# The gated-delta scan's block inverse as 32x32 and 64x64 tile products, with forward and backward heads in turn

## The chip, the cores and the metric

One core of one Trainium2 chip runs the whole program. The metric is the time of one execution in microseconds on the device. The core's engines are TensorE (PE, matrix products), VectorE (DVE), ScalarE (ACT), GpSimd (POOL) and SyncE (SP); SP and ACT also issue DMAs.

## The reference

The program is a forward pass of a small model on 256 context and 512 latent tokens of width 1024: a mixer layer with an SSD scan and a gated-delta scan in two directions, an output projection and MLP, then two further blocks with attention and gated MLPs. What matters here is the gated-delta scan (8 heads of 128, forward and backward):

```python
def gdn_scan(q, k, v, g, beta, S0, return_y):
    ...
    decay = exp(where(incl, gcum[..., :, None] - gcum[..., None, :], -inf))
    kk = einsum('bchik,bchjk->bchij', k_beta, kc) * decay
    tmat = eye(Q) + where(strict, kk, 0.0)
    rhs = concatenate([vc * bc, k_beta * exp(gcum)[..., None]], axis=-1)
    sol = triangular_solve(tmat, rhs, lower=True, unit_diagonal=True)
    ...
    def step(S, inp):
        v_new = u_i - w_i @ S
        S_next = S * d_i + kd_i^T @ v_new
        o = qd_i @ S + qk_i @ v_new
```

The kernel works in chunks of 128 tokens (6 chunks), so each head and chunk needs the inverse of a 128x128 unit triangular matrix: lower triangular for the forward direction, upper for the backward one.

## The kernel before, in words

The scan lies between the SSD scan and the output projection, from about 665 to 872 us of the span. The 16 pairs of head and direction are handled as four quads q of four heads each. Before, q = 0, 1 are the two head groups forward and q = 2, 3 the two backward. Each quad has its tiles with four 128x128 matrices side by side (128 x 512): `S` the state, `DT0`/`DT1` (one for each parity of the step t) the transposed inverse, `DB` its untransposed diagonal blocks, `C5`/`C6` the off-diagonal corners of the matrix (32x32 corners and the 64x64 corner), `PM` the negated product, `KD`, `VN`, `QE`, `QKD`, `VB` for the scan itself, and two banks of PSUM: `A[q]` for the inverse, `B[q]` for the scan. In traces `DU` is the tile of `DT0`, and `C` stands for both `C5` and `C6`.

The 32x32 diagonal blocks are inverted earlier, and come back through memory. The scan then builds the 128x128 inverse in two levels. For the first, `corner5` multiplies the 32x32 corners with the inverted diagonal blocks, ACT (`corner`) negates the result into `PM`, `block5` multiplies with the other diagonal block, and DVE (`block5`) copies and transposes the blocks that are needed into `DB` and `DT`. The second level, `corner6`, `corner`, `block6_t` and DVE's `block6_t`, does the same with 64x64 blocks. Of each product only off-diagonal blocks are needed, but all four parts call

```python
            def four(dst, w, x):
                for j in range(4):
                    o = slice(j * P, (j + 1) * P)
                    mm = pe.matmul(dst[:, o], w[:, o], x[:, o], start=True, stop=True)
                return mm
```

with whole 128x128 matrices, in which the unneeded blocks of `C5`, `C6` and `DT` are zeros that POOL wrote (`zeroed`).

The inverse of step t + 1 is built within step t. PE's order in a step t is written out by hand: per quad `state_read` and `corner5(t + 1)`; per quad `new_values` and `block5(t + 1)`; the four `output` (latent chunks, t >= 2); per quad `state_step` and `corner6(t + 1)`; per quad `key_rows(t + 1)` (transposes) and `block6_t(t + 1)`; and four `gate_rows`. Step 5, the last, builds nothing. In step 0 `square_sum` products of the SSD norm stand between the `corner5`. ACT's order is: four copies of corner 5, four `new_values`, four copies of corner 6, then `load_corners(t + 2, q)`, three DMAs per quad. DVE's is `right_side`, `block5`, `output`, `state_step`, `key_rows` with `block6_t`, `gated_query`. SP's queue loads, for each t and q, four diagonal blocks into `DT` (`load_dt`, which waits for `new_values` of step t - 2 and `corner5` of t - 1), then three into `DB` (`load_d32`, which waits for `corner6` of t - 1), and after the four quads `VB` and `QKD` for each (`load_step`; `QKD` waits for `output` of the step before, q by q). `corner5(t, q)` waits for all ten small loads of its quad: `pre_loaded[q]` counts them.

Of the kernel before, what the change touches and what calls it, by code (L numbers as in the profile page):

```python
# [18 lines left out]
P = 128  # L19
D = 1024  # L20
# [7 lines left out]
SH = 16  # L28
# [206 lines left out]
def build_kernel(nc, a, out):  # L235
    ctx = ExitStack()
    with ctx:
# [239 lines left out]
        def pair_of(q, t):  # L477

            return (q // 2 * NCH + GSEQ[q // 2][t]) * 2 + q % 2

        def lat_pair(q, t):

            return (q // 2 * (NCH - NCTX) + GSEQ[q // 2][t] - NCTX) * 2 + q % 2

        def block_at(q, t):

            if t < 4:
                return q // 2, (2 * t + q % 2) * 16
            return 2, 64 * (q // 2) + (2 * (t - 4) + q % 2) * 16
# [30 lines left out]
        def scal4(ap, w):  # L520
# [66 lines left out]
            12, 24, 24, 20, 24, 24, 24, 16, 24, 48, 3, 2, 11, 8, 8, 8, 3, 20, 20, 16, 16, 20, 20, 20, 16, 16, 24, 24, 24, 24, 65, 65, 65, 8, 32, 4)  # L587
# [56 lines left out]
        def _(sp_):  # L644
# [87 lines left out]
            for ts, ds in (((0, 1, 2, 3), (0,)), ((0, 1, 2, 3), (1,)), ((4, 5), (0, 1))):  # L732
                for d in ds:
                    for t in ts:
                        for q in (2 * d, 2 * d + 1):
# [36 lines left out]
            def load_d32(t, q):  # L772

                for r in (0, 1, 2) if q < 2 else (1, 2, 3):
                    sp_.dma_start(diagonal(DB[q][:, :], r), blocks_of(xv_dram, q, t, r)).then_inc(pre_loaded[q], 16)

            def load_step(t, q):

                d, c = q // 2, GSEQ[q // 2][t]
# [4 lines left out]
                sp_.dma_start(VB[q][:, :], v_dram[:, c * D + 512 * (q % 2):c * D + 512 * (q % 2) + 512]).then_inc(vb_loaded[q], 16)  # L784
# [17 lines left out]
            for t in range(1, NCH):  # L802
                for q in range(4):
                    if t == 4:
                        sp_.wait_ge(xb_stored, 64)
                        sp_.wait_ge(xv_stored, 64)
                    n = 4 * (t - 1) + q + 1
                    if t == 1:
                        sp_.wait_ge(zeroed, 12 + q + 1)
                    else:  # L810
                        sp_.wait_ge(dr_full, n - 4)
                    sp_.wait_ge(p5_full, n)
                    load_dt(t, q)
                    sp_.wait_ge(p6_full, n)
# [27 lines left out]
        def _(pe):  # L842
# [242 lines left out]
            def key(t, q, j):  # L1085

                h, c = 4 * (q % 2) + j, GSEQ[q // 2][t]
# [9 lines left out]
            def block5(t, q):  # L1097

                pe.wait_ge(pm_ready, 8 * t + q + 1)
                four(A[q], DT[t % 2][q], PM[q]).then_inc(e5_full, 1)  # L1100

            def corner6(t, q):

                pe.wait_ge(dt64_ready, 4 * t + q + 1)
                four(A[q], C6[q], DB[q]).then_inc(p6_full, 1)

            def block6_t(t, q):

                pe.wait_ge(pm_ready, 8 * t + 4 + q + 1)
                four(A[q], PM[q], DT[t % 2][q]).then_inc(e6t_full, 1)  # L1110
# [9 lines left out]
            def gate_rows(t, q):  # L1120
# [5 lines left out]
                pe.matmul(B[q][:, :], rowcol((GSEQ[q // 2][t] - NCTX) * 4 + q), grow[6][:, :], start=True, stop=True).then_inc(egb_full, 1)  # L1126
# [53 lines left out]
            for part in (corner5, block5, corner6, block6_t):  # L1180
                for q in range(4):
                    part(0, q)
            for t in range(NCH):
                lat, more = t >= NCTX, t < NCH - 1
                for q in range(4):
                    if t:
                        state_read(t, q)
                    if more:
                        corner5(t + 1, q)
                    if t == 0:  # L1190
                        if q == 0:
                            pe.wait_ge(kd_ready, 4)
                        for b in ((0, 1, 2), (3, 4, 5), (6, 7), ())[q]:
                            square_sum(b)
                for q in range(4):
                    if t == 0 and q >= 2:
                        pe.wait_ge(norm_ln, q - 1)
                    new_values(t, q)
# [1503 lines left out]
```

## Time and profile before

| what | value |
|---|---|
| median of 3 runs | 2569.04 us (2565.2 to 2571.09) |
| time of the profiled execution | 2571.75 us |
| its span in the profile | 2569.9 us |
| PE busy, share of the span | 94% |
| scan, step 0 to the end of step 5 | 694.64 to 871.99 us |

A span starts with the first instruction and ends with the last; the time of an execution has about 1.9 us more around it. Busy shares count instructions of products, copies and the like, not waits or the issue of DMAs. PEclk or the granted clock is the share of TensorE's full speed that it was given: 1.00 is 2.4 GHz, 0.50 is 1.2 GHz. In traces a float32 product is recorded as two passes, each with a load of the weights ahead of it (PEld), so one `four` is eight records.

### The profile page before, as it was taken

What the parts mean: (1) busy time and instruction counts of PE and PEld (TensorE: products, weight loads), DVE (VectorE), ACT (ScalarE), POOL (GpSimd) and SP (SyncE); (2) the same over time, 40 slices, a digit from 0 to 9 for tenths busy, and PEclk for the clock granted to TensorE, in tenths of its full rate; (3) what the DMA queues carried; (4) which work ended last, traced back from release to release, by engine and by line L of the source; (5) the groups of instructions that cost most, each with busy time, mean ns of one, the idle gap of its engine ahead of it and who ended that gap; (6) DMA issues with size and microseconds to landing.
All of it is one profiled execution on the core that took longest, in us unless ns stands there. A gap on an engine that the chain in (4) does not pass through costs nothing.

```text
span 2569.9 us, 30397 instructions
## 1 busy us (share of the span) xinstructions
PE 2406.2 (94%) x12022; PEld 1942.5 (76%) x12022; DVE 1364.3 (53%) x2161; ACT 1020.2 (40%) x1687; POOL 153.9 (6%) x116
## 2 busy tenths in 40 slices
PE   3899899978899998999999899999999899999997
PEld 2788787734699876888887668888888667888885
DVE  8566774488566534444445654434344554444445
ACT  3544457623432554233255354222235354322222
POOL 0000000000000010000031301000002301000002
PEclk9999999965799999999999999999999999999998
DMA  5233425511343422222232202222223201222222
GB/s 237 99 123 123 164 83 164 190 32 38 89 115 92 152 82 84 99 98 99 91 106 74 66 1 78 97 97 98 99 88 108 66 25 42 98 99 96 93 98 82
DMA packets 124477, 248.29 MB, mean 97 GB/s; under 512 B 58096, under 2 KB 58864, under 8 KB 123568
## 3 DMA queue, kind: packets, MB, share of 16 engines
q1 hardware_dynamic: 106320, 234.02, 27.7%
q10 hardware_dynamic: 18016, 12.33, 1.6%
q8 instruction: 96, 1.57, 0.3%
q14 instruction: 45, 0.37, 0.0%
HBM read 221.13 MB, written 25.17 MB: 96 GB/s over the span
## 4 chain that ended last, share of the span: by engine, by line
PE 81%; DVE 8%; ACT 4%; DMA 3%; issue 2%; ACTq 0%; SPq 0%; POOL 0%; DVEq 0%
PE bank L1219 18%; PE bank L1221 18%; PE bank L1220 18%; PE bank L1082 4%; PE bank L928 4%; PE bank L1379 3%; PE bank L1370 2%; DMA raw<-in_s_qkvx 2%; DVE cacc L2020 2%; PE bank L927 1%; PE bank L392 1%; PE bank L1405 1%; PE bank L394 1%; PE bank L393 1%; DMA modw<-in_w_mod 1%
## 5 line engine op out<-in xcount | busy, mean ns | idle before, releaser
L1666 ACT ACTIVATE whi<-raw 128x1024 fp32r<-128x1024 f32 (+1 forms) x267 | 277.7, 1041 | 927.8 <-PE bank L1221 923.2
L1219 PE MATMUL bank<-ahi,whi 128*128 128x512 f32 x1152 | 454.9, 395 | 9.1 <-DVE alo L2421 6.0
L1220 PE MATMUL bank<-alo,whi 128*128 128x512 f32 x1152 | 451.2, 392 | 0.0
L1221 PE MATMUL bank<-ahi,wlo 128*128 128x512 f32 x1152 | 450.9, 391 | 0.0
L2303 DVE TENSOR_TENSOR wlo<-raw,whi 128x1024 fp32r<-128x1024 f32 (+1 forms) x267 | 326.3, 1222 | 135.4 <-ACT whi L1666 134.9
L1219 PE MATMUL bank<-bhi,whi 128*128 128x512 f32 x736 | 286.8, 390 | 0.0
L1221 PE MATMUL bank<-bhi,wlo 128*128 128x512 f32 x736 | 286.6, 389 | 0.0
L1220 PE MATMUL bank<-blo,whi 128*128 128x512 f32 x736 | 286.6, 389 | 0.0
L1219 PEld LDWEIGHTS bank<-ahi,whi 128*128 128x128 f32 x1152 | 218.0, 189 | 59.2 <-issue 10.6
L1221 PEld LDWEIGHTS bank<-ahi,wlo 128*128 128x128 f32 x1152 | 217.9, 189 | 45.7
L1220 PEld LDWEIGHTS bank<-alo,whi 128*128 128x128 f32 x1152 | 217.8, 189 | 45.8 <-issue 1.4
L2636 POOL TENSOR_TENSOR accx<-accx,sqr 128x512 f32<-128x512 f32 x42 | 72.3, 1721 | 1603.8 <-ACT sqr L1734 1379.7
L1219 PEld LDWEIGHTS bank<-bhi,whi 128*128 128x128 f32 x736 | 138.2, 188 | 28.8 <-issue 0.3
L1221 PEld LDWEIGHTS bank<-bhi,wlo 128*128 128x128 f32 x736 | 138.3, 188 | 28.6
L1220 PEld LDWEIGHTS bank<-blo,whi 128*128 128x128 f32 x736 | 138.3, 188 | 28.6
L2379 DVE TENSOR_TENSOR xr<-bank,xr 128x512 f32<-128x512 f32 x64 | 44.3, 691 | 157.1 <-PE bank L1221 157.1
L409 DVE TENSOR_TENSOR wlo<-raw,whi 128x1024 fp32r<-128x1024 f32 x51 | 62.3, 1222 | 99.2 <-ACT whi L402 98.9
L402 ACT ACTIVATE whi<-raw 128x1024 fp32r<-128x1024 f32 x51 | 54.4, 1068 | 146.6 <-DMA raw<-in_s_qkvx 84.2
L928 PE MATMUL bank<-hhi,whi 128*128 128x512 f32 x272 | 109.8, 404 | 0.0
L928 PE MATMUL bank<-hlo,whi 128*128 128x512 f32 x272 | 109.0, 401 | 0.0
L928 PE MATMUL bank<-hhi,wlo 128*128 128x512 f32 x272 | 108.8, 400 | 0.0
L2020 DVE SCALAR_TENSOR_TENSOR cacc<-cbuf,vec,cacc 128x784 f32<-128x784 f32 (+1 forms) x102 | 98.2, 963 | 10.7 <-ACT cacc L1521 8.0
(421 smaller groups left out, 3974.9 us busy)
## 6 DMA issues: line engine op xcount, KB each, us to landing
raw<-in_s_gu SPq DMA_DIRECT2D x88, 512.0 KB, 3.2
raw<-in_s_qkvx SPq DMA_DIRECT2D x34, 512.0 KB, 4.8
late_modw<-in_w_mod SPq DMA_DIRECT2D x32, 512.0 KB, 3.8
raw<-in_s_up SPq DMA_DIRECT2D x32, 512.0 KB, 3.2
raw<-in_s_down SPq DMA_DIRECT2D x32, 512.0 KB, 3.2
raw<-in_s_dn SPq DMA_DIRECT2D x32, 512.0 KB, 3.2
raw<-in_s_win SPq DMA_DIRECT2D x24, 512.0 KB, 3.2
raw<-in_s_zg SPq DMA_DIRECT2D x16, 512.0 KB, 4.0
```

Of the source, the lines that this page charges most:

```text
L402: act.activation(whi[k][:, 0:kc * P], raw[k][:, 0:kc * P], ACT.Identity).then_inc(hi_ready, 1)
L409: dve.tensor_tensor(wlo[k][:, 0:kc * P], raw[k][:, 0:kc * P], whi[k][:, 0:kc * P].bitcast(F32), ALU.subtract).then_inc(lo_ready, 1)
L928: mm = pe.matmul(lat, w, x[:, s, CTX:TOK], start=first, stop=last)
L1082: mm = pe.matmul(dst[:, o], w[:, o], x[:, o], start=True, stop=True)
L1219: pe.matmul(out, w_hi, x_hi, start=start, stop=False)
L1220: pe.matmul(out, w_hi, x_lo, start=False, stop=False)
L1221: return pe.matmul(out, w_lo, x_hi, start=False, stop=stop)
L1379: mm = pe.matmul(bank[4 + (h // 2) % 2][64 * (h % 2):64 * (h % 2) + 64, qb * P:(qb + 1) * P], vh[:, kb_ * LAT + h * 64:kb_ * LAT + (h + 1) ...
L1666: act.activation(whi[u % 2][:, 0:width[u + 2] * P], raw[u % 2][:, 0:width[u + 2] * P], ACT.Identity).then_inc(hi_ready, 1)
L2020: after(dve.scalar_tensor_tensor(out=acc, in0=x, scalar=w, in1=acc, op0=ALU.mult, op1=ALU.add))
L2303: dve.tensor_tensor(wlo[u % 2][:, 0:width[u + 2] * P], raw[u % 2][:, 0:width[u + 2] * P], whi[u % 2][:, 0:width[u + 2] * P].bitcast(F32), ...
L2636: pool.tensor_tensor(acc[:, :], acc[:, :], sqr[n % 2][:, :], ALU.add).then_inc(sq_added, 1)
```

## The change

All quads are renumbered: q = 0, 2 are now forward and q = 1, 3 backward (q % 2 is the direction, q // 2 the head group). The four inverse parts of PE are issued for pairs of quads p, (0, 1) and (2, 3), one forward and one backward. The first level is made of eight products 32x32 by 32x32 per quad, the second of four 64x64 by 64x64, and the products of the two quads of a pair alternate. As the two directions use opposite corners, neighbouring products lie on different row and column groups of the array. ACT's copy of the second corner covers only its 64x64 blocks. `C5` and `C6` are no longer zeroed, so their loads don't wait for it. SP fetches the `DT` blocks of all four quads before the `DB` blocks of any.

```diff
+            def blocks32(first, w, x, full, p):
+                for j in range(4):
+                    for i in range(2):
+                        for q in (2 * p, 2 * p + 1):
+                            a, b = (2 * i, 2 * i + 1) if q % 2 == 0 else (2 * i + 1, 2 * i)
+                            k, m = (a, b) if first else (b, b)
+                            rows, out = slice(32 * k, 32 * k + 32), slice(32 * b, 32 * b + 32)
+                            mc, nc_ = slice(j * P + 32 * m, j * P + 32 * m + 32), slice(j * P + 32 * a, j * P + 32 * a + 32)
+                            mm = pe.matmul(A[q][out, nc_], w[q][rows, mc], x[q][rows, nc_], start=True, stop=True)
+                            if j == 3 and i == 1:
+                                mm.then_inc(full, 1)
-            def corner5(t, q):
-                pe.wait_ge(pre_loaded[q], 160 * (t + 1))
-                if t:
-                    pe.wait_ge(dt_ready, 4 * (t - 1) + q + 1)
-                four(A[q], C5[q], DB[q]).then_inc(p5_full, 1)
+            def corner5(t, p):
+                for q in (2 * p, 2 * p + 1):
+                    pe.wait_ge(pre_loaded[q], 160 * (t + 1))
+                    if t:
+                        pe.wait_ge(dt_ready, 4 * (t - 1) + q + 1)
+                blocks32(True, C5, DB, p5_full, p)
...
+            def quadrants(upper, w, x, full, p):
+                for j in range(4):
+                    for q in (2 * p, 2 * p + 1):
+                        k, m = (slice(0, 64), slice(64, 128)) if (q % 2 == 0) == upper else (slice(64, 128), slice(0, 64))
+                        kc, mc = slice(j * P + k.start, j * P + k.stop), slice(j * P + m.start, j * P + m.stop)
+                        mm = pe.matmul(A[q][m, kc], w[q][k, mc], x[q][k, kc], start=True, stop=True)
+                        if j == 3:
+                            mm.then_inc(full, 1)
...
                 if more:
-                    for q in range(4):
-                        state_step(t, q)
-                        corner6(t + 1, q)
-                    for q in range(4):
+                    for p in range(2):
+                        state_step(t, 2 * p)
+                        state_step(t, 2 * p + 1)
+                        corner6(t + 1, p)
+                    for p in range(2):
...
             for t in range(1, NCH):
...
                 for q in range(4):
-                    n = 4 * (t - 1) + q + 1
...
                     load_dt(t, q)
-                    sp_.wait_ge(p6_full, n)
+                for q in range(4):
+                    sp_.wait_ge(p6_full, 4 * (t - 1) + q + 1)
                     load_d32(t, q)
...
             def corner(t, q, full):
                 act.wait_ge(full, 4 * t + q + 1)
-                act.activation(PM[q][:, :], A[q][:, :], ACT.Identity, scale=-1.0).then_inc(pm_ready, 1)
+                src, dst = h4(A[q][:, :]), h4(PM[q][:, :])
+                if full is p6_full:
+                    r, c = (slice(64, 128), slice(0, 64)) if q % 2 == 0 else (slice(0, 64), slice(64, 128))
+                    src, dst = src[r, :, c], dst[r, :, c]
+                act.activation(dst, src, ACT.Identity, scale=-1.0).then_inc(pm_ready, 1)
...
             for q in range(4):
-                act.wait_ge(zeroed, 4 + 2 * (q + 1))
                 load_corners(0, q)
...
-            for q in range(4):
-                for t in (C5, C6):
-                    pool.memset(t[q][:, :], 0.0).then_inc(zeroed, 1)
```

DVE's `key_rows` and `block6_t` also go by pairs: two `key_rows`, then two `block6_t`. In step 0 five `square_sum` follow the first pair's `corner5` and three the second's.

## Rows read from the trace of the kernel before

**Rows 1.** The page: span, busy time of TensorE, granted clock in 40 slices.

```profile
span 2569.9 us, 30397 instructions
PE 2406.2 (94%) x12022; PEld 1942.5 (76%) x12022; DVE 1364.3 (53%) x2161; ACT 1020.2 (40%) x1687; POOL 153.9 (6%) x116
PEclk9999999965799999999999999999999999999998
```

**Rows 2.** Stretches: length, busy us of each engine, granted clock, DMA share, GB/s.

```profile
676.20:694.60 18.40, 17.42 (x128) 17.07 (x129) 8.38 (x21) 8.81 (x16) 0.00 (x0) 0.85 0.39 89
694.64:724.69 30.05, 30.05 (x227) 26.23 (x225) 16.23 (x32) 16.34 (x32) 0.00 (x0) 1.00 0.30 62
724.69:753.19 28.50, 28.12 (x247) 27.41 (x245) 18.28 (x56) 9.23 (x24) 0.00 (x0) 1.00 0.60 184
753.19:788.60 35.41, 35.10 (x308) 34.58 (x309) 22.25 (x61) 9.33 (x24) 0.00 (x0) 1.00 0.34 84
857.68:871.99 14.31, 14.31 (x128) 14.31 (x129) 10.95 (x28) 9.01 (x25) 0.00 (x0) 1.00 0.59 200
640.00:660.00 20.00, 19.64 (x112) 10.92 (x110) 16.28 (x46) 9.61 (x33) 0.00 (x0) 0.50 0.01 1
```

**Rows 3.** Timeline of PE in step 2: start us, us, line, what, count.

```profile
774.73 1.06 PE L1082 MATMUL bank<-VN,KD 128*128 128x128 f32 x8
775.62 1.06 PE L1082 MATMUL bank<-DB,C 128*128 128x128 f32 x8
...
787.12 1.18 PE L1126 MATMUL bank<-grow,rowsel 128*128 128x512 f32 x4
788.60 1.16 PE L1137 MATMUL bank<-S,kf 128*128 128x128 f32 x8 [0.31 <-DVE QE L2261]
```

**Rows 4.** Timeline of ACT's DMA issues at the end of step 2.

```profile
782.08 1.20 ACTq L1674 DMA_DIRECT2D C<-at_scratch  x2
...
789.20 0.62 ACTq L1676 DMA_DIRECT2D C<-at_scratch  x1
```

**Rows 5.** Timeline of SP's DMA issues behind step 2's outputs, first and last.

```profile
775.41 1.74 SPq L770 DMA_DIRECT2D DU<-xb_scratch  x4
...
789.97 1.57 SPq L775 DMA_DIRECT2D DB<-xv_scratch  x3
```

**Rows 6.** DMA issues from 665 to 870: count, size, median us to landing.

```profile
C<-at_scratch ACTq DMA_DIRECT2D x24, 64.0 KB, 2.4
DB<-xv_scratch SPq DMA_DIRECT2D x72, 16.0 KB, 2.1
```

**Rows 7.** Timelines of PE and ACT between steps 0 and 1.

```profile
719.37 0.60 PE L1117 MATMUL bank<-cf,kf 128*128 128x128 f32 x4
719.81 1.06 PE L1082 MATMUL bank<-DT,PM 128*128 128x128 f32 x8
...
731.18 1.16 PE L1082 MATMUL bank<-DB,C 128*128 128x128 f32 x8
...
719.58 1.20 ACTq L1674 DMA_DIRECT2D C<-at_scratch  x2
```

**Rows 8.** Timeline of PE in attention, one of its rounds.

```profile
1489.57 0.60 PE L1405 MATMUL bank<-cf,eb 128*128 128x128 f32 x4
1490.10 1.09 PE L1379 MATMUL bank<-pt,vh 128*64 128x128 f32 x8
1491.12 1.13 PE L1370 MATMUL bank<-kh,qh 128*128 128x512 f32 x2
```

**Rows 9.** Timeline of PE at half clock: SSD tiles, and the first `corner5`.

```profile
646.85 1.12 PE L1069 MATMUL bank<-cpm,hst 64*64 64x128 f32 x8
...
676.23 6.37 PE L1082 MATMUL bank<-DB,C 128*128 128x128 f32 x32 [7.55 <-DMA DB<-xv_scratch]
```

**Rows 10.** Timelines of ACT and PE around the start of step 0.

```profile
692.99 0.60 ACT L1650 ACTIVATE PM<-bank 128x512 f32<-128x512 f32 x1 [1.37 <-issue]
...
695.53 2.74 PE L1171 MATMUL bank<-zs,cf 128*128 128x512 f32 x6
```

More of the change, by code:

```diff
@@ new lines, in corner5, with block5 @@
+            def corner5(t, p):
[4 more added lines that the diff above has]
+                blocks32(True, C5, DB, p5_full, p)
+            def block5(t, p):
+                for q in (2 * p, 2 * p + 1):
+                    pe.wait_ge(pm_ready, 8 * t + q + 1)
+                blocks32(False, DT[t % 2], PM, e5_full, p)
+            def quadrants(upper, w, x, full, p):
+                for j in range(4):
+                    for q in (2 * p, 2 * p + 1):
+                        k, m = (slice(0, 64), slice(64, 128)) if (q % 2 == 0) == upper else (slice(64, 128), slice(0, 64))
[3 more added lines that the diff above has]
+                            mm.then_inc(full, 1)
@@ L1112, in key_rows, with corner6, block6_t @@
+            def corner6(t, p):
+                for q in (2 * p, 2 * p + 1):
+                    pe.wait_ge(dt64_ready, 4 * t + q + 1)
+                quadrants(True, C6, DB, p6_full, p)
+            def block6_t(t, p):
+                for q in (2 * p, 2 * p + 1):
+                    pe.wait_ge(pm_ready, 8 * t + 4 + q + 1)
+                quadrants(False, PM, DT[t % 2], e6t_full, p)
             def key_rows(t, q):
@@ L1180, in _ @@
             for part in (corner5, block5, corner6, block6_t):
-                for q in range(4):
-                    part(0, q)
+                for p in range(2):
+                    part(0, p)
             for t in range(NCH):
                 lat, more = t >= NCTX, t < NCH - 1
-                for q in range(4):
+                for p in range(2):
                     if t:
-                        state_read(t, q)
+                        state_read(t, 2 * p)
+                        state_read(t, 2 * p + 1)
                     if more:
-                        corner5(t + 1, q)
+                        corner5(t + 1, p)
                     if t == 0:
-                        if q == 0:
+                        if p == 0:
                             pe.wait_ge(kd_ready, 4)
-                        for b in ((0, 1, 2), (3, 4, 5), (6, 7), ())[q]:
+                        for b in (range(5), range(5, KB))[p]:
                             square_sum(b)
-                for q in range(4):
-                    if t == 0 and q >= 2:
-                        pe.wait_ge(norm_ln, q - 1)
-                    new_values(t, q)
+                for p in range(2):
+                    for q in (2 * p, 2 * p + 1):
+                        if t == 0 and q >= 2:
+                            pe.wait_ge(norm_ln, q - 1)
+                        new_values(t, q)
                     if more:
-                        block5(t + 1, q)
+                        block5(t + 1, p)
                 if lat:
@@ L1204, in _ @@
                 if more:
-                    for q in range(4):
-                        state_step(t, q)
-                        corner6(t + 1, q)
-                    for q in range(4):
+                    for p in range(2):
+                        state_step(t, 2 * p)
+                        state_step(t, 2 * p + 1)
+                        corner6(t + 1, p)
+                    for p in range(2):
                         if t + 1 < NCH - 1:
-                            key_rows(t + 1, q)
-                        block6_t(t + 1, q)
+                            key_rows(t + 1, 2 * p)
+                            key_rows(t + 1, 2 * p + 1)
+                        block6_t(t + 1, p)
                     if t + 1 >= NCTX:
@@ L2338, in _ @@
                         state_step(t, q)
-                    for q in range(4):
+                    for p in range(2):
                         if t + 1 < NCH - 1:
-                            key_rows(t + 1, q)
-                        block6_t(t + 1, q)
+                            key_rows(t + 1, 2 * p)
+                            key_rows(t + 1, 2 * p + 1)
+                        block6_t(t + 1, 2 * p)
+                        block6_t(t + 1, 2 * p + 1)
                     if t + 1 >= NCTX:
```

74 lines of the change are left out of this document (32 added, 42 removed).

## The prediction, written before the changed kernel ran

> **What bounds the kernel now.** I read the page first. TensorE (PE) is busy for 94% of the span, and the granted clock is near full speed except around slices 9 to 11 [rows 1]. The change sits in one stage, the gated-delta scan, so next I read busy time by stretches [rows 2]. In a scan step with output (753.19 to 788.60, 35.41 us) PE is busy for 35.10 us, VectorE (DVE) for 22.25, ScalarE (ACT) for 9.33: the scan is bound by PE. The timeline shows the unit of that work: one call of `four`, recorded as eight matmul passes, takes 0.89 us start to start (774.73 to 775.62) [rows 3]. A step has 28 such units (four quads q by seven parts), another eight in the output part (7.15 us), four groups of transposes of 0.44 us (719.37 to 719.81 [rows 7]) and the gate rows (1.4 us up to the next state read [rows 3]): 25.0 + 7.15 + 1.8 + 1.4 = 35.3. Sixteen of the units, 14.3 us, are the four inverse parts that the change touches.
>
> Then I read what else has to be ready. Two queues carry the small block loads. ACT issues twelve loads of corners behind its last corner copy: 782.08 to 789.82, 7.7 us [rows 4]. SyncE (SP) issues 28 loads of blocks, starting 0.7 us after the last output product: 775.41 to 791.54, 16.1 us [rows 5]. One lands 2.1 to 2.4 us after its issue [rows 6]. In step 1 the corner loads start at 719.58 and the last `corner5` starts at 731.18, 11.6 us later, just when the last load has landed [rows 7]. The queues are already as long as the PE work that covers them.
>
> **The change part by part.** *The products.* A `four` is four 128x128 products. `blocks32` makes eight products of 32x32 by 32 instead for each quad, `quadrants` four of 64x64 by 64. For a pair of quads that is 32 and 16 recorded passes. No row shows a tile of this size in turn with others, so the pace is bounded. A full-size pass takes 0.112 us (0.89 over eight). A tile with a quarter of the columns to load and to stream would at proportion take 0.028. Two tiles in turn halve the pace: eight passes of the 64x64 products of the stage before last 1.12 us at half clock, about 0.10 us each once the tail of the last is taken off, where the full-size ones at that clock take 0.20 (32 in 6.37 us) [rows 9]. So 0.014 is the lower bound (size and turn both pay) and 0.056 the upper (only the turn pays). I take 0.032 for the 32-blocks, near proportion, since the smaller a pass the more a fixed cost shows; and 0.043 for the quadrants, midway between 0.028 and 0.056.
>
> Going in and out of tiles costs too. In attention, four transposes next to tiled products take 0.53 us (1489.57 to 1490.10) and the eight 128*64 passes 1.02 (to 1491.12) [rows 8], against 0.44 and 0.89 in the scan [rows 3, 7]: 0.22 us together, with a little more at the wide product behind. I take 0.3 us for each pair part, bounds 0.2 and 0.4. So a pair of 32-block parts costs P = 32 x 0.032 + 0.3 = 1.3 us (bounds 0.65 and 2.2) and a pair of quadrants Q = 16 x 0.043 + 0.3 = 1.0 (0.4 and 1.3), both against 1.79 before. A step needs 4P + 4Q = 9.2 us where it had 14.3.
>
> The Trainium skill, "TensorE: Matmul & The Clock Gate" (Step-by-step, decode and dispatch), speaks against the change: without hardware decode each matmul costs about 62 ns at the sequencer. By that estimate P would be 32 x 0.062 + 0.3 = 2.3 us and the gain of the 32-blocks gone; the 0.10 us at half clock in rows 9 neither shows nor excludes it. The same page's floor with hardware decode, about 25 ns, would make P 1.1.
>
> *The copies.* The ACT copy of the second corner shrinks from 128x512 to 64x256 (0.60 to about 0.45 us). Two of them now come together after a pair, so the corner loads start some 0.4 us later behind the last product than before. The DVE copies are the same, and DVE has 13 us of a step free [rows 2]. With two `block6_t` copies behind a pair, QE comes about 0.4 us later than the 0.31 us PE already waits for it [rows 3].
>
> *The loads.* Number and size stay. The DT loads of all quads now stand ahead of all DB loads. From step 3 on SP can't start them before the last QKD load of the step before, which waits for the last output product. So the chain stays 0.7 + 16.1 + 2.1 = 18.9 us from the last output product to the second pair of `corner5`; the first pair needs 22 of the 28 loads, 14.2 us. The ACT chain is 12.0 us from the last quadrant product to the second `corner5` pair (11.8 from 719.37 to 731.18 [rows 7], plus 0.2 for the second copy). Eight POOL memsets of C go; they ran while PE waited for the first DB load (until 676.23 [rows 9]), so they give nothing. If that cover were gone they would be worth the time by which the first C loads lag the first DB load, which is none.
>
> *Start.* The first `corner5` still waits for its DB load. Before, the clock there was 0.85 over 18.4 us [rows 2], that is 5.5 us at half and full from then on. Now PE has little to do between the copies, so it stays half: P 2.3, Q 1.7. From 676.2 on, `corner5` ends at 680.8, `block5` at 685.4, `corner6` at 689.2. The ACT copies of corner 6 then go one by one with three corner loads behind each (three issues of 0.65 us are 1.97), as before, where the last came at 692.99 [rows 10]; mine comes at 693.1, and step 0 at 695.4 against 694.64. Step 0: P 2.3 at half clock, five wide products (0.43 us per pass, six in 2.58 [rows 10]; the first three at half clock) to 704.4, then P, 2.6, 3.6 + 2P, 3.6 + 2Q: last `corner6` ends at 720.1, against 719.4. PE work saved, 5 us, is paid back by the half clock and ACT.
>
> *Steps.* Step 1: second `corner5` at 720.1 + 12.0 = 732.1; PE itself would be there 8.7 us after 720.1 (transposes 1.8, 2Q, four state reads 3.6, P), so it waits 3.3 us. Then P + 3.6 + 2P + 3.6 + 2Q = 13.1: 745.2. Step 2: 757.2 (wait 1.4), then P + 3.6 + 2P + 7.15 = 14.65: output ends 771.9 (before 774.73). Steps 3 and 4: 18.9 + 14.65 = 33.55 us each instead of 35.41, with 2.7 us of waiting in each: output ends at 805.4 and 839.0 (before 774.73 + 2 x 35.41 = 845.6). Then 5.6 for states and corners, 2.0 for `block6_t`, 1.4 gate rows, 0.7 for QE: the reads of the last step start at 848.7, before at 857.68 [rows 2]. Step 5 and what follows has no inverse part and moves along. If the clock holds, the scan is 9.0 us shorter: of the 31 us of PE work that six rounds lose (6 x 5.1), 10.1 turn into waits for loads, the rest goes at the start and in the half clock.
>
> **The clock is what I doubt.** In the stage ahead of the scan PE is busy 19.64 of 20 us and its granted clock is 0.50 (1.2 GHz) [rows 2]; what runs there are mostly 128*64 and 64*64 tiles. In the scan, with 128*128 tiles, it is 1.00. So small tiles keep PE busy on record without bringing the clock back. (The skill's same page, Part 1, has the clock follow how busy PE has been; by "busy" as recorded, that stage should be at full clock, and it is not.) The changed scan puts waits of 1 to 3 us right next to 32*32 products, four times. I expect the clock to fall there in most steps, and to come back in the next run of full-size products (at the start it was back about 5.5 us after full-size work began). A dip that lasts over the next four full-size units (3.6 us) costs half its length or more, about 2 us, less what falls in a wait: 1.5 us x 4 = 6 us.
>
> **Sum.** 9.0 - 6 = 3.0 us less. The profiled execution took 2571.75 us (a span of 2569.9 and 1.9 around it), 2.7 above the median of the runs; 2568.7 there is 2566.0 at the median of 2569.04.
>
> **Rivals.** *A, the clock holds.* For it: the scan before keeps 1.00 throughout and two thirds of its PE work stays full-size. Against: the row at 0.50. Result: 9.0 less with my P and Q, 2552 to 2562, centre 2560; both lower bounds at once would take off 16 x 0.65 + 8 x 0.6 = 15 us more, which needs every unknown at its best end. *B, the forecast*: dips in most steps, 2561 to 2571. *C, slow small passes*: if a 32-block pass takes 0.056 us or more, P = 2.1 to 2.3; 16 P lie on the path worked out above, so 16 x 0.8 = 12.8 us come back: 3.8 us slower with the clock held, 9 with some dips, 2573 to 2578. It decides the sign once a pass takes more than 0.050 us (0.032 + 9.0/512), or 0.038 with the dips of B. (The 62 ns of the skill's "TensorE: Matmul & The Clock Gate", cited above, would be this case.) *D, the clock stays down* (the other side): once it falls at the wait in step 1, NV, S and the tiled parts up to the outputs of step 2 run at half clock: 14.4 us more for full-size work (16 units of 0.9), 5 x 1.0 for P and 4 x 0.7 for Q, less 4.7 in waits: 17.5 us; and 5 us each in steps 3 and 4 up to the outputs. 27.5 - 9.0 = 18 us slower, 2587, and 2576 to 2600 as it lasts shorter or longer. *E, the loads bind anyway*, or the change does nothing: only if the small products were free would PE wait longer; the chains above already hold them, so the loads limit a gain and can't cancel it.
>
> **Numbers.** A 0.33 (faster); B 0.37, of it 0.07 faster by over 0.2%, 0.23 within, 0.07 slower; C 0.12 (0.04 within, 0.08 slower); D 0.18 (slower). 0.2% is 5.1 us, and about what a measurement of this kernel tells from no change. Faster 0.40, same 0.27, slower 0.33. B is the likeliest: 2566.0, its own range 2561 to 2571. The range for 8 in 10 takes in A down to 2553 and the near half of D: 2553 to 2584.
>
> **What would show it.** Right: `corner5` groups of 32 passes within 1.0 us and `quadrants` of 16 within 0.7; PE idle ahead of the second `corner5`, released by the C load in steps 1 and 2 and by the DB load in 3 and 4; 33 to 35 us from output to output; a granted clock under 1.00 in the stretches from 690 to 702 and around 730. Wrong: PE busy without gaps (C), clock 1.00 throughout (A), or 0.50 over several tens of us (D). The forecast falls most easily by the clock, next by the pace of a 32-block pass.

## The result, and the profile after

| | median us | runs | ratio to before, 95% |
|---|---|---|---|
| before | 2568.74 | 4 | |
| changed | 2553.58 | 4 | 0.9939 [0.9924, 0.9954] |

The changed kernel is 15.2 us (0.6%) faster. The forecast was 2566.0, 3 us less than before. The sign came out as forecast and the time lies 0.6 us inside the lower end of the range (2553), so the size has to be explained: the gain is five times the forecast one. The profiled execution took 2555.91 us, 15.84 less than the one before (2571.75). One execution of `no_turns` below took 4687.05 us, and the ratio given there leaves it out.

The page of the changed kernel (compare [rows 1]):

```profile
span 2554.1 us, 31191 instructions
PE 2360.5 (92%) x12406; PEld 1883.5 (74%) x12406; DVE 1364.3 (53%) x2161; ACT 1013.2 (40%) x1687; POOL 148.5 (6%) x108
PEclk9999999975589999999999999999999999999998
```

PE is busy for 45.7 us less, the span is 15.8 us shorter: two thirds of the work saved turned into idle time. The clock is low for longer, slices 9 to 12 read 7, 5, 5, 8 where [rows 1] has 6, 5, 7, 9. The stretches that answer to [rows 2] show where. Each row: start and end, length, busy us (instructions) of PE, PEld, DVE, ACT and POOL, granted clock, DMA share, GB/s. They are the start, steps 0, 1, 2, 3 and 4; from step 1 on a step runs from its first state read to the next step's:

```profile
678.47:694.72 16.25, 6.81 (x192) 5.86 (x193) 8.21 (x21) 7.82 (x16) 0.00 (x0) 0.50 0.43 92
694.72:719.71 24.99, 23.85 (x288) 16.88 (x288) 13.68 (x29) 15.27 (x32) 0.00 (x0) 0.89 0.24 58
719.71:751.80 32.09, 23.51 (x313) 20.75 (x309) 18.93 (x58) 8.14 (x24) 0.00 (x0) 0.79 0.58 169
751.80:779.23 27.43, 26.43 (x373) 24.25 (x373) 21.35 (x61) 8.00 (x24) 0.00 (x0) 1.00 0.42 104
779.23:809.63 30.40, 26.57 (x372) 24.30 (x372) 21.44 (x61) 8.02 (x24) 0.00 (x0) 1.00 0.41 99
809.63:840.71 31.08, 25.79 (x357) 23.93 (x357) 19.02 (x57) 8.13 (x24) 0.00 (x0) 0.95 0.38 104
```

Against [rows 2] the start is 2.2 us shorter although PE is at half clock all through it, step 0 is 5.1 us shorter, step 1 is 3.6 us longer, and step 2 is 8.0 us shorter (35.41 to 27.43). Steps 3 and 4 give 5.0 and 2.6 (before 35.4 and 33.7). In steps 2 and 3 PE does the same work, 26.4 and 26.6 us; what differs is its idle time. From the first `corner5` to the last step's state reads the scan is 19.2 us shorter. The profiled execution gains only 15.8, because the scan began 2.2 us later in it and what follows took 1.2 us longer; neither is explained here.

The timeline of PE in step 2 shows the price of the small products (start, length, engine, line, operation, out<-in, tile, shape, count, then idle time and its releaser). L1164 is the state reads, L1099 `blocks32`, L1123 `quadrants`, L1082 `four`:

```profile
751.80 2.05 PE L1164 MATMUL bank<-S,kf 128*128 128x128 f32 x16 [1.00 <-DVE QE L2295]
753.78 0.45 PE L1099 MATMUL bank<-DB,C 32*32 32x32 f32 x32
754.16 2.05 PE L1164 MATMUL bank<-S,kf 128*128 128x128 f32 x16
756.14 0.45 PE L1099 MATMUL bank<-DB,C 32*32 32x32 f32 x32
...
770.38 0.68 PE L1123 MATMUL bank<-DB,C 64*64 64x64 f32 x16
771.00 2.05 PE L1082 MATMUL bank<-VN,KD 128*128 128x128 f32 x16
```

Thirty-two passes of the blocks take 0.38 us start to start (753.78 to 754.16), sixteen of the quadrants 0.62 (770.38 to 771.00). A part of the way in and out of tiles is in the full-size group behind: two units take 1.98 (754.16 to 756.14), not 1.79. So P is 0.58 us and Q 0.81. The prediction had 1.3 and 1.0, with 0.65 as P's lower bound. QE is late by 1.00 us, 0.7 more than the 0.31 in [rows 3].

PE in step 1, where time is lost, and the two queues beside it:

```profile
724.58 0.65 PE L1099 MATMUL bank<-DB,C 32*32 32x32 f32 x32 [2.81 <-DMA DB<-xv_scratch]
725.15 3.78 PE L1164 MATMUL bank<-S,kf 128*128 128x128 f32 x16
733.60 0.65 PE L1099 MATMUL bank<-DB,C 32*32 32x32 f32 x32 [4.67 <-DMA DB<-xv_scratch]
734.18 3.75 PE L1082 MATMUL bank<-VN,DT 128*128 128x128 f32 x16
...
719.27 7.12 SPq L775 DMA_DIRECT2D DB<-xv_scratch  x12
726.44 1.20 SPq L784 DMA_DIRECT2D VB<-v_scratch  x1
...
725.18 0.61 ACTq L1752 DMA_DIRECT2D y_scratch<-yfm  x1
```

The issue of the last DB load ends at 726.4 and PE is released at 733.6, 7 us later, where the median landing before was 2.1 us [rows 6]. A store of 2 MB (725.18) and eight loads of 256 KB (VB and QKD, from 726.44) share the transfer engines with it, whose busy share over 724.2 to 737.8 is 0.94. The second `corner5` stands at 733.60 instead of 731.18 [rows 7]. Behind the first wait PE's groups take 3.78 instead of 2.05: the clock has fallen to half, and it is still there behind the second.

Steps 3 and 4, PE around `corner5`, and SP's loads of step 3 (compare [rows 5]):

```profile
783.89 0.45 PE L1099 MATMUL bank<-DB,C 32*32 32x32 f32 x32 [2.61 <-DMA DB<-xv_scratch]
...
786.55 0.45 PE L1099 MATMUL bank<-DB,C 32*32 32x32 f32 x32 [0.22 <-DMA DB<-xv_scratch]
786.93 2.05 PE L1082 MATMUL bank<-VN,DT 128*128 128x128 f32 x16
...
814.28 0.45 PE L1099 MATMUL bank<-DB,C 32*32 32x32 f32 x32 [2.60 <-DMA DB<-xv_scratch]
...
818.40 0.45 PE L1099 MATMUL bank<-DB,C 32*32 32x32 f32 x32 [1.68 <-DMA DB<-xv_scratch]
818.78 2.97 PE L1082 MATMUL bank<-VN,DU 128*128 128x128 f32 x16
821.68 0.65 PE L1099 MATMUL bank<-PM,DT 32*32 32x32 f32 x32
822.26 2.44 PE L1082 MATMUL bank<-VN,DU 128*128 128x128 f32 x16
...
769.18 9.13 SPq L770 DMA_DIRECT2D DU<-xb_scratch  x16
778.37 6.73 SPq L775 DMA_DIRECT2D DB<-xv_scratch  x12
```

The state products of step 2 begin at 768.50, right behind the last output product. SP issues from 769.18 on for 15.9 us, and the second `corner5` starts 18.05 us after that product; in step 4 it is 19.5 us (798.91 to 818.40). The chain of loads sets the pace, and it is about as long as forecast (18.9). Step 3 keeps the full clock through a wait of 2.61 us; step 4 loses it after waits of 2.60 and 1.68, and its groups then take 2.97, 0.65 and 2.44 instead of 2.05, 0.45 and 2.05, 1.5 us in all.

### The profile page after: what moved, and what is told of

It reads as the page before. It is cut to its first block, busy times and chain, and to the rows that moved or that the text cites. A ratio compares the mean times of both kernels' runs of the same rounds, so it can differ in the third digit from the quotient of the medians.

```text
span 2554.1 us, 31191 instructions
## 1 busy us (share of the span) xinstructions
PE 2360.5 (92%) x12406; PEld 1883.5 (74%) x12406; DVE 1364.3 (53%) x2161; ACT 1013.2 (40%) x1687; POOL 148.5 (6%) x108
## 4 chain that ended last, share of the span: by engine, by line
PE 79%; DVE 8%; ACT 4%; DMA 4%; issue 3%; SPq 3%; POOL 0%; DVEq 0%; ACTq 0%
PE bank L1250 18%; PE bank L1251 18%; PE bank L1252 18%; PE bank L928 4%; PE bank L1410 3%; PE bank L1401 2%; DVE cacc L2054 1%; DMA raw<-in_s_qkvx 1%; PE bank L927 1%; SPq L770 1%; PE bank L392 1%; PE bank L1082 1%; PE bank L1436 1%; PE bank L394 1%; PE bank L393 1%
## 5 line engine op out<-in xcount | busy, mean ns | idle before, releaser
L1252 PEld LDWEIGHTS bank<-ahi,wlo 128*128 128x128 f32 x1152 | 217.8, 189 | 45.7
L1252 PEld LDWEIGHTS bank<-bhi,wlo 128*128 128x128 f32 x736 | 138.2, 188 | 28.6
L1251 PEld LDWEIGHTS bank<-blo,whi 128*128 128x128 f32 x736 | 138.2, 188 | 28.6
```

What stands on the lines that cost most here:

```text
L1251: pe.matmul(out, w_hi, x_lo, start=False, stop=False)
L1252: return pe.matmul(out, w_lo, x_hi, start=False, stop=stop)
```

## The experiments

All are edits of the changed kernel. Theory: the small products cost almost nothing on PE, and what is left is set by the loads. The first rivals were that the order of loads or heads gives the gain, and that the turn between forward and backward heads does. Beside the ratio I give, from each profile, the length of the scan from the first `corner5` to the last step's state reads, in parts: to the first state reads, then steps 1 to 4. The start of the scan itself moves by several us between executions (670.3 to 679.1), and these lengths leave that out; but they are of one execution each, and where the clock dips differs between executions.

| kernel | ratio to before, 95% | start + step 0 | 1 | 2 | 3 | 4 | sum us |
|---|---|---|---|---|---|---|---|
| before | 1 | 48.5 | 28.5 | 35.4 | 35.4 | 33.7 | 181.4 |
| changed | 0.9939 [0.9924, 0.9954] | 41.2 | 32.1 | 27.4 | 30.4 | 31.1 | 162.2 |
| whole_products | 1.0026 [1.0016, 1.0036] | 50.3 | 32.0 | 35.4 | 35.4 | 33.7 | 186.8 |
| first_level_only | 0.9924 [0.9910, 0.9939] | 43.0 | 27.7 | 30.6 | 30.8 | 30.4 | 162.5 |
| twice | 0.9977 [0.9968, 0.9987] | 43.2 | 33.1 | 30.6 | 32.5 | 30.8 | 170.2 |
| no_turns | 0.9949 [0.9934, 0.9963] | 42.0 | 33.6 | 28.6 | 34.7 | 30.1 | 168.9 |
| old_load_order | 0.9948 [0.9934, 0.9963] | 39.6 | 33.6 | 31.0 | 32.1 | 28.4 | 164.7 |
| spill_late | 0.9936 [0.9922, 0.9949] | 39.9 | 26.4 | 31.7 | 31.3 | 29.6 | 158.9 |
| dt_ahead | 0.9896 [0.9882, 0.9910] | 39.6 | 33.6 | 27.6 | 27.4 | 25.2 | 153.4 |
| first_level_dt_ahead | 0.9933 [0.9919, 0.9947] | 42.7 | 29.7 | 30.6 | 30.6 | 28.8 | 162.4 |
| dt_ahead_spill_late | 0.9899 [0.9882, 0.9915] | 40.8 | 26.5 | 34.8 | 28.7 | 25.1 | 156.0 |
| all_three | 0.9928 [0.9914, 0.9941] | 42.5 | 24.9 | 33.2 | 30.6 | 28.8 | 160.0 |
| qkd_last | 0.9928 [0.9911, 0.9944] | 39.9 | 33.8 | 31.0 | 31.1 | 28.8 | 164.6 |
| qkd_last_spill_late | 0.9890 [0.9869, 0.9912] | 40.4 | 26.9 | 30.9 | 29.3 | 27.5 | 155.1 |

**1. whole_products.** The order of loads and heads without the small products.

```diff
-                blocks32(True, C5, DB, p5_full, p)
+                for q in (2 * p, 2 * p + 1):
+                    four(A[q], C5[q], DB[q]).then_inc(p5_full, 1)
```

and so for the three other parts; C5 and C6 are zeroed and both ACT copies are whole, as before. These two go back together with the products; no run takes them apart.

> The changed kernel with all four inverse parts as whole 128x128 products again (the corners' buffers zeroed, both ACT copies whole); the heads in turn, the pairs and the order of the loads stay. Theory 1, the small products carry the gain: it goes back to the kernel before, 14 to 17 us slower than the changed one. Theory 2, the gain comes from the order of the loads or of the heads: it keeps at least half, 0 to 8 us slower than the changed one.

Measured: 2575.93 us, ratio 1.0026, 22 us slower than the changed kernel and 7 slower than before. Theory 1 holds more than fully: the small products, with what goes with them, are worth all of the gain and repay a loss of 7 us that the new order of heads, pairs and loads brings. Steps 2 to 4 last as before to a tenth, so the order is neutral there. The loss is at the start and in step 1:

```profile
695.83 3.05 PE L1082 MATMUL bank<-DU,PM 128*128 128x128 f32 x16 [1.91 <-ACT PM L1685]
...
736.90 3.14 PE L1082 MATMUL bank<-DB,C 128*128 128x128 f32 x16 [2.01 <-DMA C<-at_scratch]
```

Two quads wait together for the later of their copies or loads (1.91 us where the old order had 0.80), and both waits are followed by groups at a lower clock (3.05 and 3.14 for 1.95). That the pairs cause this loss is read from these rows; no run has the pairs alone.

**2. first_level_only.** Quadrants as whole products, blocks small.

```diff
-                quadrants(True, C6, DB, p6_full, p)
+                for q in (2 * p, 2 * p + 1):
+                    four(A[q], C6[q], DB[q]).then_inc(p6_full, 1)
```

> The changed kernel with the 64x64 quadrants as whole products again; the 32x32 blocks stay small. It adds 4.0 us of PE work to each step (4 pairs of parts, 1.79 for 0.8). Theory 1, what lies between the last output product and the first corner5 is covered by the loads: the waits of steps 1, 3 and 4 (7.5, 2.8 and 4.3 us) take it in, only step 2 and the start show it: 4 to 7 us slower than the changed kernel. Theory 2, all PE work counts: 18 to 20 us slower.

Measured: ratio 0.9924, not slower than the changed kernel at all, and a scan of 162.5 against 162.2. The direction of theory 1 was right (PE work behind the outputs is hidden by the loads, theory 2 is out), its 4 to 7 us were not. The row of the table shows why: step 2 costs 3.1 us more, the start and step 0 1.8, but step 1 is 4.4 us shorter. There the first pair doesn't wait, the second waits 2.81 us instead of 4.67, and the clock holds until then:

```profile
718.71 0.45 PE L1099 MATMUL bank<-DB,C 32*32 32x32 f32 x32
...
723.96 0.45 PE L1099 MATMUL bank<-DB,C 32*32 32x32 f32 x32 [2.81 <-DMA C<-at_scratch]
724.34 2.76 PE L1082 MATMUL bank<-VN,DT 128*128 128x128 f32 x16
```

Half of the change, the 64x64 level, was worth nothing that could be measured in this kernel.

**3. twice.** The small products issued two times over; the last product of the second round increments the semaphore.

```diff
-                for j in range(4):
+                for j, last in [(j, False) for j in range(4)] + [(j, j == 3) for j in range(4)]:
```

> The changed kernel with each small product issued twice, one round after the other, so that the pace of a pass shows as a duration without the way in and out of tiles. Theory 1, a 32-block pass takes 0.012 us and a quadrant pass 0.03 to 0.04: the groups of a pair grow by 0.4 and 0.55 us, the kernel by 8 to 12 us (what is not in waits for loads). Theory 2, the pace of the prediction (0.032 and 0.043): 1.0 and 0.7 us a pair, 18 to 24 us.

Measured: ratio 0.9977, 10 us slower than the changed kernel (scan 8.0). The pace by itself, in step 2:

```profile
756.30 0.76 PE L1099 MATMUL bank<-DB,C 32*32 32x32 f32 x64
756.99 2.05 PE L1164 MATMUL bank<-S,kf 128*128 128x128 f32 x16
...
774.80 1.15 PE L1123 MATMUL bank<-DB,C 64*64 64x64 f32 x32
775.88 2.05 PE L1082 MATMUL bank<-VN,KD 128*128 128x128 f32 x16
```

Thirty-two more block passes add 0.31 us (0.38 to 0.69), 0.010 a pass; sixteen more quadrant passes add 0.46 (0.62 to 1.08), 0.029 a pass. The prediction's 0.032 and 0.043 are out, its lower bound for the blocks (0.014) too. What is left of one round, 0.07 us of 0.38 and 0.16 of 0.62, comes once a group, and I count it with the way in and out: with the 0.2 in the full-size group that makes 0.27 and 0.35 us.

**4. no_turns.** All products of the forward quad, then all of the backward one.

```diff
-                for j in range(4):
-                    for i in range(2):
-                        for q in (2 * p, 2 * p + 1):
+                for q in (2 * p, 2 * p + 1):
+                    for j in range(4):
+                        for i in range(2):
...
```

and the same in `quadrants`.

> The changed kernel with the small products of a pair not in turn: all of the forward quad, then all of the backward one. Theory 1, the turn between disjoint parts of the array halves a pass: P grows by 0.4 us and Q by 0.5, on the path 16 x 0.4 and some 0.5s: 6 to 12 us slower than the changed kernel. Theory 2, the small size alone gives the pace and the turn nothing: within 1.5 us.

```profile
756.07 0.60 PE L1099 MATMUL bank<-DB,C 32*32 32x32 f32 x32
756.60 2.05 PE L1164 MATMUL bank<-S,kf 128*128 128x128 f32 x16
...
773.27 0.96 PE L1123 MATMUL bank<-DB,C 64*64 64x64 f32 x16
774.16 2.05 PE L1082 MATMUL bank<-VN,KD 128*128 128x128 f32 x16
```

A pair of block parts takes 0.53 instead of 0.38, one of quadrants 0.89 instead of 0.62. So turns shorten the parts, as theory 1 has it, by 4 x 0.15 + 4 x 0.27 = 1.7 us of PE work a step. In the time it shows as 0.9949 against 0.9939, about 2.6 us and within the intervals, below theory 1's 6 to 12 and above theory 2's 1.5. (The profiled execution took 2561.2 us, 5 above the median, and its scan is long by that.) Over a whole group the quadrants take 0.89/16 = 0.056 us a pass without turns and 0.62/16 = 0.039 with them, the blocks 0.53/32 = 0.017 and 0.38/32 = 0.012. 0.056 is half of a full-size pass for half the columns, so size gives proportion and the turn takes about a third off. (The 0.029 and 0.010 of `twice` are for an added pass; without turns no run shows that.) The blocks without turns are at 0.017, not 0.028. The likely reason, argued from the code: even then the loop over i goes back and forth between two disjoint blocks of one quad.

**5. old_load_order.**

```diff
                     load_dt(t, q)
-                for q in range(4):
                     sp_.wait_ge(p6_full, 4 * (t - 1) + q + 1)
                     load_d32(t, q)
```

> The changed kernel with SP's loads quad by quad again, DT then DB of each. Theory 1, the new order helps only where DT can run while corner6 of the step isn't done, in steps 0 and 1: there the last load comes 1 to 4 us later; from step 3 on the same 28 loads follow the last output product in either order and the second pair waits for the last of them as before: 0 to 5 us slower than the changed kernel. Theory 2, the new order carries the gain: 10 us slower or more.

Measured: 0.9948, 2 us slower with overlapping intervals, scan 164.7. Theory 1; in step 1 the second `corner5` (724.48) waits 8.38 us, in the changed kernel 4.67. Fetching all DT blocks first gives 2 us or nothing.

**6. spill_late.** The 2 MB store of y is issued behind the `corner5` copies of step 1.

```diff
                         corner(t + 1, q, p5_full)
+                        if t == 1 and q == 3:
+                            act.wait_ge(yn_ready, KB)
+                            act.dma_start(y_dram, yfm[:, :]).then_inc(y_spilled, 16)
...
-                if t == 0:
-                    act.wait_ge(yn_ready, KB)
-                    act.dma_start(y_dram, yfm[:, :]).then_inc(y_spilled, 16)
```

> The changed kernel with the 2 MB store of y behind the corner5 copies of step 1 instead of ahead of them. The last DB load of step 1 was issued at 726.4 and released PE at 733.6, 7 us where the median is 2.2. Theory 1, the store's traffic delays it: the wait of 4.67 us shrinks to 2 or less and the clock comes back earlier, 2 to 4 us faster than the changed kernel. Theory 2, the VB and QKD loads of 256 KB behind it on SP's queue do that: the wait stays above 3.5 us.

```profile
725.04 0.65 PE L1099 MATMUL bank<-DB,C 32*32 32x32 f32 x32
...
746.44 0.45 PE L1099 MATMUL bank<-DB,C 32*32 32x32 f32 x32 [2.46 <-DMA DB<-xv_scratch]
...
728.12 13.20 SPq L770 DMA_DIRECT2D DT<-xb_scratch  x16
```

The wait of 4.67 us is gone (725.04 has none) and step 1 lasts 26.4 us instead of 32.1, so the store was the cause; the VB and QKD loads, which are still there (from 722.55), don't make this wait without it. The wait ahead of the first pair stays, at 3.19 us for 2.81. But the ratio hardly moves (0.9936, 1.6 us by the medians where 2 to 4 were expected). The store now meets the DT loads of the next step, whose issue takes 13.20 us instead of 9.1 to 9.3, and the time comes back as a wait in step 2 (31.7 instead of 27.4).

**7. dt_ahead.** The DT loads of step t+1 ahead of the QKD loads of step t on SP's queue.

```diff
                 for q in range(4):
                     load_step(t, q)
+                if t < NCH - 1:
+                    transposed(t + 1)
+                for q in range(4):
+                    load_qkd(t, q)
```

`load_step` keeps the VB load alone, `transposed` holds the DT loads with their waits, and `load_qkd` the QKD load, which waits for the output product of the step before.

> The changed kernel with the DT loads of step t+1 issued ahead of the QKD loads of step t, so that they no longer wait for the last output product. Theory 1, the loads set the pace of steps 3 and 4: the chain behind the last output product loses 9.1 us (16 DT loads), the waits of 2.8 and 4.3 us go, and with them the dip of the clock in step 4 (1.5 us), until PE itself or ACT's corner loads bind: 6 to 9 us faster than the changed kernel. Theory 2, the waits only change their releaser (ACT's corner loads, the QKD loads that now come later): within 2 us.

SP and PE in step 3:

```profile
785.78 9.20 SPq L770 DMA_DIRECT2D DT<-xb_scratch  x16
795.02 1.85 SPq L791 DMA_DIRECT2D QKD<-qk_scratch  x4
798.75 7.23 SPq L775 DMA_DIRECT2D DB<-xv_scratch  x12
...
783.80 0.45 PE L1110 MATMUL bank<-DB,C 32*32 32x32 f32 x32
784.19 2.05 PE L1093 MATMUL bank<-VN,DT 128*128 128x128 f32 x16
```

Measured: 2542.64 us, ratio 0.9896, 11 us faster than the changed kernel (6 to 9 were expected). No wait for a load is left from step 2 on, the clock is 1.00 there, and steps 2 and 3 last 27.6 and 27.4 us. That checks P and Q once more: without inverse parts a step has 12 units (10.7), outputs 7.15, transposes 1.8, gate rows 1.4 and 0.7 more for QE, 21.8 us; 27.4 - 21.8 leaves 5.6 for 4P + 4Q, and 4 x 0.58 + 4 x 0.81 is 5.6.

**8. first_level_dt_ahead.** Edits 2 and 7 together.

> Whole products for the second level, small ones for the first, DT loads ahead of QKD. Theory, the second level's small products gave nothing because its 4.0 us a step lay in the waits for loads: with these gone they count in steps 2, 3 and 4, less 0.7 each for QE, 8 to 10 us more than with small quadrants there; at the start and in step 1 whole quadrants give 2 to 3 us back (clock, landing). Together 5 to 8 us slower than DT ahead with all products small. If the second level's products don't matter even without the waits: within 2 us.

Measured: 0.9933, 9 us slower than edit 7 alone, and 162.4 us of scan against 153.4. The small quadrants that were worth 0.3 us of scan behind the old queue order are worth 9.0 behind the new one. This is the plainest proof that the loads held the gain back.

**9. dt_ahead_spill_late and all_three.** Edits 6 and 7, without and with edit 2.

> DT loads ahead of QKD and the store of y late together, all products small. If the two waits are independent, the scan from the first corner5 to the last state reads takes the 66.3 us of the run with the late store up to step 2 and the 80.2 us of the run with DT ahead behind it: 146.5 instead of 153.4 and 162.2, 5 to 7 us faster than DT ahead alone. If the time saved in step 1 comes back as a wait for DB in step 2 (2.46 us with the late store alone), 3 to 4 us faster. If step 1 stays as it is with DT ahead (a wait of 7 us that the 256 KB loads cause), no gain.

> Small 32x32 blocks, whole products for the second level, DT loads ahead of QKD, the store of y late. With whole quadrant products a step with output has 4.0 us more PE work and no waits in reach: steps of 30.4 us bound by PE (25.0 + 7.15 + 1.8 + 1.4 less 4 x 1.2 for corner5 and block5), 2547 to 2551. If the clock at the start and in step 1 decides, it comes out faster than the changed kernel with DT ahead alone; if PE work decides, it is slower by 3 to 6 us.

PE's wait in step 2 of the first:

```profile
751.51 0.65 PE L1110 MATMUL bank<-DB,C 32*32 32x32 f32 x32 [5.28 <-DMA DB<-xv_scratch]
```

Measured: 0.9899 and 0.9928. Step 1 gets its 7 us (26.5 for 33.6), and step 2 gives them back (34.8 for 27.6, with a wait of 5.28 us for DB): of the first expectation's cases it is nearest the second, but the whole gain came back, not half. all_three is slower than the same kernel with small quadrants by 4 us and than edit 7 by 6 by the medians (7 and 8 by the ratios, 4.0 and 6.6 by the scan): its PE work decided, not the better clock of its step 1.

**10. qkd_last and qkd_last_spill_late.** Edit 7 with the DB loads ahead of QKD too, without and with edit 6.

> DT ahead of QKD, and now DB too: QKD is the last of a step's small queue. With DT ahead alone there were no waits for loads from step 2 on, so nothing is left to gain there; step 1, with its 7.26 us behind the store of y, has the same loads in the same order. Expected: within 2 us of DT ahead alone. Rival: the outputs now wait for their QKD loads, 2 to 5 us slower.

> The same with the store of y late. In the run with DT ahead and the late store PE waited 5.28 us in step 2 for DB loads that stood behind four QKD loads (2.58 us) on SP's queue. Without these ahead the wait falls to about 2.7 us: 2 to 3 us faster than that run, 2541 to 2543. Rival: the DT loads slowed by the store (13.5 us for 16 instead of 9.2) set the time of the first DB load, and the wait stays near 5 us.

```profile
752.77 0.45 PE L1113 MATMUL bank<-DB,C 32*32 32x32 f32 x32 [2.04 <-DMA C<-at_scratch]
753.15 3.18 PE L1096 MATMUL bank<-VN,DU 128*128 128x128 f32 x16
...
745.09 2.58 SPq L791 DMA_DIRECT2D QKD<-qk_scratch  x4
749.12 3.53 SPq L784 DMA_DIRECT2D VB<-v_scratch  x4
...
747.85 0.62 ACTq L1725 DMA_DIRECT2D C<-at_scratch  x1
```

Measured: 0.9928 and 0.9890. The first is 9 us slower than edit 7, which neither expectation had. It isn't the outputs that wait, it is `corner5`, for a corner load. The likely reason, only argued here: QKD and VB, 2 MB together, now follow each other (745.1 to 752.7) while the corner loads of the second pair, the last issued from 747.9 to 748.5, are in flight. PE is released at 752.77, 4.3 us later (the median before was 2.4 [rows 6]), and behind a wait of 2.04 us comes a group of 3.18 instead of 2.05: wait and half clock make 3.5 us a step, three times. The second is 2 us faster than edits 6 and 7 together, as expected (step 2 takes 30.9 us instead of 34.8), though the intervals overlap, and ends level with edit 7 alone: 2542.74 and 2542.64 us, the best two of the study, 10 to 11 us below the changed kernel and not to be told apart.

## Why the prediction was right in sign and wrong in size

- **The products: the step that failed.** P = 1.3 and Q = 1.0 should have been 0.58 and 0.81. A quadrant pass was put at 0.043, between 0.028 and 0.056; an added one takes 0.029. A 32-block pass was put at 0.032, near proportion, for fear of a fixed cost; an added one takes 0.010, and the runs show a fixed cost for a group (0.07 us), not for a pass. That is below the lower bound of 0.014 too. The likely reason is that the bound counted one turn, between the quads, where the loop has two: four disjoint blocks follow each other. The way in and out was right: 0.27 and 0.35 us where 0.3 was put. 4P + 4Q is 5.6 us, not 9.2.
- Decode doesn't bound it: two recorded passes make one product, so a product of the blocks takes 0.38/16 = 0.024 us, 0.019 by the run with two rounds. The Trainium skill, "TensorE: Matmul & The Clock Gate" (Step-by-step, decode and dispatch), has about 62 ns for each matmul without hardware decode. The same page of the Trainium skill (Back-to-back issue gap) has about 25 ns as the issue floor. The trace excludes the first for this kernel; the second is met or slightly undercut if a matmul is a product, and undercut by half if it is a recorded pass.
- **The start and step 0.** Forecast 47.7 us from the first `corner5` to the first state reads (676.2 to 723.9), measured 41.2. Half clock at the start was right. Three us fall in the start, where the four block parts at half clock take 0.65 instead of 2.3 each and PE waits between them; 3.5 are the four P and four Q of step 0 (3.6 by the sum).
- **Step 1.** The wait was forecast as 3.3 us behind C loads. It is 2.81 and 4.67 behind DB loads. The store of y makes the second (edit 6); without it the first is still there. From the first state reads to the second `corner5` it took 13.9 us where 8.2 were forecast: 4.2 of waits and the rest state reads at half clock. The landing time had been taken as a constant of 2.1 to 2.4.
- **Steps 2 to 4.** The load chain of 18.9 us measured 18.05 and 19.5. The tail behind it, P + 3.6 + 2P + 7.15, is 12.5 instead of 14.65, since it holds three P. With the chain about right and the tail too long, a step came out as 33.55 where it was 30.4 between the ends of the outputs of steps 2 and 3 (768.50 to 798.91), and 33.4 to step 4's, with the dip.
- **The clock.** Forecast: dips in most steps, 6 us. Measured: one behind the waits of step 1 (3.75 for 2.05, 0.2 on a block part, 1.9 us; what it costs ahead of the second wait, that wait takes in) and one in step 4 (1.5), none in steps 2 and 3: 3.4 us. The price of a dip was right, their number wasn't. The run with QKD last has three of them, each behind a wait of about 2 us (1.92 to 2.05). Which waits bring one isn't settled: 2.61 us in step 3 didn't, and in qkd_last_spill_late waits of 1.83 and 2.27 us left the clock at 1.00 in steps 3 and 4. Small products aren't needed for one: whole_products has none, and its groups behind waits of 1.91 and 2.01 us took 3.05 and 3.14 for 1.95.
- **By part.** Forecast from the first `corner5` on: 47.7, 27.2, 32.3, 33.5 and 31.8 us for the columns of the table, and 6 for dips, 178.5 in all. Measured: 41.2, 32.1, 27.4, 30.4 and 31.1, dips included, 162.2. The products and the dips made the sum too long, step 1 made it too short by 4.9. That the time still fell into the range, by 0.6 us, is luck: by this sum, with step 1 as forecast, it would have been below.
- **The signs named.** The groups were as short as asked (0.45 and 0.68 us), and the clock was low at both places named. The releaser in step 1 was a DB load, not C; step 2 had no wait for a load; and from output to output it was 30.4 and 33.4 us, not 33 to 35 in both.
- **Slips that the sum doesn't rest on.** The first pair of `corner5` was put 14.2 us behind the last output product; 0.7 + 22 x 0.575 + 2.1 is about 15.4, and 15.4 was measured (768.50 to 783.89). Q's lower bound of 0.4 takes 0.014 a pass, where the quadrants' own was 0.028. A full-size pass at half clock is 0.22 us; 32 in 6.37 mixes both clocks, as the prediction's own 5.5 us at half clock say. QE was put 0.4 us later in the words and 0.7 in the sum; 0.7 came.
- **Rivals.** The time is that of A (2552 to 2562), but not by A: the clock did fall. It is B's mechanism at about half its price, with P and Q below A's. C and D are excluded by rows. E was worded too weakly: the loads didn't cancel the gain, but PE waits for them for 14.6 us in steps 1 to 4, and edit 7 gives 11 us back.
- What stays open: the differences between the changed kernel, first_level_only, old_load_order and no_turns in whole time lie within their intervals; only the scan lengths of one execution each tell them apart.

## What to carry to other kernels

When PE work shrinks in a stage whose queues are already as long as its cover, price the queue first, and ask for each load what it waits behind: here four QKD loads that waited for an output held up sixteen loads whose own waits had long been over. Test each half of a change again once the bound has moved; the quadrants were worth nothing before and 9 us after. Ask also what flies beside a load: here the wait moved with the 2 MB store, from step 1 to step 2.

## What the runs showed of the hardware that wasn't expected

- Products of 32x32 by 32 in f32 ran at 0.024 us each (16 in 0.38 us), forward and backward blocks in turn, and at 0.033 (16 in 0.53) one quad after the other; those of 64x64 at 0.078 (8 in 0.62) and 0.111 (8 in 0.89).
- More disjoint blocks in turn meant a shorter pass, over a whole group: 0.056 and 0.039 us for 64x64 (one and two blocks in turn), 0.017 and 0.012 for 32x32 (two and four). An added pass took 0.029 and 0.010 in `twice`.
- Going from full-size products to these and back cost 0.2 us in the full-size group behind and 0.07 (32x32) or 0.16 us (64x64) in the small group itself.
- A 16 KB load took 7 us to land beside a 2 MB store, for a median of 2.1, and 16 DT loads took 13.2 us to issue instead of 9.2 with it in flight.
- The granted clock fell to half (1.2 GHz) behind waits of 1.92 to 2.81 us next to small products in some steps, and stayed full (2.4 GHz) around ones of 2.61 and 2.27 in others. It also fell behind waits of 1.91 and 2.01 us where all products around were full-size (whole_products).
